# The opening stage of a two-block transformer kernel: modulation units summed in pairs per chunk on VectorE and GpSimd, sine arguments kept in PSUM, the first norm made chunk by chunk, the first two weight blocks interleaved

## The chip, the cores and the metric

One core of a Trainium2 chip runs the whole program. The metric is the device time of one execution in microseconds (us); three executions of the kernel before gave 2504.7, 2506.18 and 2512.43, median 2506.18.

## The reference, cut to what matters

Two transformer blocks run one after the other on 256 tokens of width 1024. Everything that the change touches lies ahead of the first large product:

```
mod   = silu(c) @ w_ada + b_ada                       # 9 x 1024 numbers; shift, scale, gate, ...
h     = x * rsqrt(mean(x*x) + eps) * norm_ffn1        # first RMS norm
h     = h * (1 + scale) + shift                       # modulate
x     = x + 0.5 * gate * ((silu(h @ w_g) * (h @ w_u)) @ w_down)
...
h     = sin(freq * (emb @ fw1 + fb1)); h = sin(freq * (h @ fw2 + fb2)); h = sin(freq * (h @ fw3 + fb3))
taps  = (h @ fw4) * window                            # filter of the second block's long convolution
```

## The kernel before

Features lie on the partitions: x is eight chunks of 128 features by 256 tokens (tile X). All 290 weight blocks go through one pipeline with two slots. SyncE loads block n into `raw[n % 2]`, ScalarE copies it to `whi` (the high part, `hi_static` and `hi_loop`), VectorE or GpSimd writes `wlo = raw - whi` (`lo_static`, `lo_loop`, `block_lo`), and TensorE makes three products per chunk and half (`three`: whi x Yh, whi x Yl, wlo x Yh). A block of the first product, `b1_gu1` (22 blocks), is 8 chunks x 2 halves x 3 = 48 matmuls of 256 columns into `pg[n % 2]`. The semaphore `lo_ready` counts finished low parts, `pe_block` finished blocks on TensorE, `dve_evac` evacuated ones. Block n + 2 is loaded once the low part of block n is done, and TensorE begins it once its low part is done and block n is evacuated.

The modulation vector is made in units: a unit is 128 of its numbers, a 128x1024 load of w_ada (tile ADA in the opening, `ada` later), multiplied by silu(c) spread over the partitions (bank px[1], with a copy CS in SBUF for GpSimd, which doesn't reach PSUM) and summed along the row. Units 0 to 7 are the shift and 8 to 15 the scale of the first norm, one per chunk. Sixteen units are loaded and summed in the opening: twelve on VectorE (`first_units`, one instruction and a small addition), four multiplied on GpSimd and summed on ScalarE (`unit_sum`). `ada_used` counts the units that are done, and SyncE waits for it before it loads unit 16 and later ones. In the queue of SyncE the load of unit 16 stands directly ahead of the load of weight block 2, and unit 17 ahead of block 3.

Order in the opening before: TensorE spreads silu(c), makes three small filter layers (`pe.matmul` into pg[0]; VectorE reduces each sine's argument to within pi in tile FA, ScalarE takes the sine), eight sums of squares, the filter's last layer (4 matmuls of 512 columns, weights FW4), the spread of the inverse root, and then blocks 0 and 1 one after the other. VectorE sums its twelve units between the sine arguments, weights the taps (tile HN), makes the low part of block 0, and after all units the eight chunks of the norm: a scaled chunk in TMP, the high part YhB on ScalarE, the low part YlB on VectorE. Each engine works through its own list in the written order.

Of the kernel before, what the change touches and what calls it, by code (L numbers as in the profile page):

```python
# [20 lines left out]
P = 128  # L21
D = 1024
SEQ = 256
N_FF = 2816
KD = D // P
KF = N_FF // P
EPS = 1e-6
F32 = mybir.dt.float32
# [49 lines left out]
POOL_UNITS = (9, 11, 12, 13)  # L78
DVE_UNITS = (0, 1, 2, 3, 4, 5, 6, 7, 8, 10, 14, 15)
# [112 lines left out]
def two_blocks(nc, x_t, ctx_t, vec, w_t, w_d, w_ada, emb_t, fw1, fw23, fw4, window, dft, rope1, sgu_w, sgu_b,  # L192
# [59 lines left out]
    at[0] = region + 43776  # L252
    ADA0 = sb("ADA0", [P, 11, KD * P])
    ADA1 = nc.alloc_sbuf_tensor_at("ADA1", [P, 4, KD * P], F32, offset=y_at)
    ADA2 = nc.alloc_sbuf_tensor_at("ADA2", [P, KD * P], F32, offset=yl_at)

    def first_unit(n):
        if n < 11:
            return ADA0[:, n, :]
        return ADA1[:, n - 11, :] if n < 15 else ADA2[:, :]  # L260

# [74 lines left out]
    with ExitStack() as ctx:  # L336
# [49 lines left out]
        def _(sp):  # L386
# [8 lines left out]
            for n in range(ADA_FIRST):  # L395
                sp.dma_start(first_unit(n), w_ada[n, :, :]).then_inc(sem[f"ada_first{n // 2}"], 16)
# [50 lines left out]
            def load(name):  # L447
# [26 lines left out]
                if not rate:  # L474
                    with sp.Fori(0, blocks // 2) as j:
                        weights(j, 0)
                        weights(j, 1)
                    return
# [24 lines left out]
        def _(pool):  # L503
# [66 lines left out]
            for k, n in enumerate(POOL_UNITS):  # L570
                if k == 0:
                    pool.wait_ge(sem["c_kept"], 1)
                pool.wait_ge(sem[f"ada_first{n // 2}"], 32)
                pool.tensor_tensor(first_unit(n), first_unit(n), CS[:, :], ALU.mult).then_inc(sem["pool_unit"], 1)
            pool.dma_start(DF0, dft[:, 0:2].rearrange("p a b n -> p (a b) n")).then_inc(sem["dft_in"], 16)
            pool.wait_ge(sem["taps_used"], 1)
            pool.wait_ge(sem["lo_ready"], CREDIT + 2)
# [8 lines left out]

            def block_lo(n):

                pool.wait_ge(sem["hi_ready"], n + 1)
                for q in range(4):  # L590
                    part = slice(512 * q, 512 * q + 512)
                    ins = pool.tensor_tensor(wlo[:, n % 2, part], raw[:, n % 2, part], whi[:, n % 2, part].bitcast(F32), ALU.subtract)
                ins.then_inc(sem["lo_ready"], 1)
# [66 lines left out]
        def _(act):  # L660
# [49 lines left out]
            def norm(name, chunks_of, tokens, shift, post, following=None):  # L710

                r, base, k = NORMS[name]
                if name not in SUMMED_NORMS and name != "b1_0":
# [10 lines left out]
                if name == "b1_0":  # L724
                    unit_sum(2)
                    hi_static(0, BLK)
                    unit_sum(3)
                    hi_static(1, BLK)
# [74 lines left out]

            for t, src in ((EMB, emb_t), (FW1, fw1), (FW23, fw23)):
                act.dma_start(t[:], src).then_inc(sem["filter_in"], 16)
            act.dma_start(FW4[:], fw4).then_inc(sem["fw4_in"], 16)
            act.dma_start(X[:, 0:4, 0:256], x_t[:, 0:4, :]).then_inc(sem["x_in"], 16)
            act.dma_start(X[:, 4:8, 0:256], x_t[:, 4:8, :]).then_inc(sem["x_more_in"], 16)
# [3 lines left out]
            act.dma_start(WIN[:], window).then_inc(sem["window_in"], 16)  # L812
            act.wait_ge(sem["c_spread"], 1)
            act.activation(CS[:, :].rearrange("p (a n) -> p a n", a=2), px[1][:, :, :], ACT.Copy).then_inc(sem["c_kept"], 1)

            def unit_sum(k):

                n, total = POOL_UNITS[k], small[:, 40 + k:41 + k]
# [3 lines left out]
                act.activation(MOD[:, n, 0:1], total, ACT.Identity, bias=V[:, VEC["b_mod"] + n:VEC["b_mod"] + n + 1])\  # L822
                    .then_inc(sem["unit_done"], 1)
# [6 lines left out]
            for layer in range(3):  # L830
                act.wait_ge(sem["sine_arg"], layer + 1)
# [2181 lines left out]
```

## Time and profile before

| | |
|---|---|
| time of the runs (median of 3) | 2506.18 us |
| span of the profiled execution, first to last instruction | 2496.1 us |
| what lies around the span, by that median | 10.1 us |
| TensorE busy | 2414.6 us (97%) |
| VectorE, ScalarE, GpSimd busy | 1516.9, 892.0, 380.6 us |
| first matmul of weight block 0 | at 48.6 us |

The profile has no total of its own for the profiled execution beside its span; the difference to the median of the runs is taken as what lies around the span. A time "at 48.6 us" is counted from the span's start. A row of the timeline gives start, duration, engine, source line, operation and tiles; in brackets stands how long the engine was idle before it, and what released it.

### The profile page before, as it was taken

To read this page: it belongs to the slowest core of one execution; us is meant where nothing else is said; L and a number is where in the kernel's file an instruction comes from. 1 tells how busy PE (TensorE), PEld (TensorE's weight loads), DVE (VectorE), ACT (ScalarE), POOL (GpSimd) and SP (SyncE) were. 2 spreads that over 40 slices of the span, in tenths; PEclk is the share of its full clock that TensorE was granted. 3 is DMA by queue.
4 is the path that set the end of the run, shared out by engine and by line. 5 is a ranking of instruction groups with operands and counts; after the bars stand their busy time and mean duration, and the time that the engine had idled before them with its cause. 6 is when DMAs were issued, how large, how long until landed. Compare 5 with 4: busy or idle time off the path is not lost.

```text
span 2496.1 us, 39335 instructions
## 1 busy us (share of the span) xinstructions
PE 2414.6 (97%) x14736; PEld 2134.7 (86%) x14736; DVE 1516.9 (61%) x2434; ACT 892.0 (36%) x1103; POOL 380.6 (15%) x353
## 2 busy tenths in 40 slices
PE   5998989999999998999999999999999999999999
PEld 4998879999888888867788888888888889999999
DVE  7767768977878665355478776652222274565544
ACT  3443554454222223432232222242222241344443
POOL 2110531211111102332201110101111000000110
PEclk9999989999999999999999999999999999999999
DMA  7878736854655554211125555522222342125455
GB/s 267 282 265 284 266 133 212 276 197 169 219 183 195 181 168 147 81 64 51 68 102 205 189 178 189 178 87 101 97 80 91 103 147 83 68 102 186 168 182 171
DMA packets 79878, 400.19 MB, mean 160 GB/s; under 512 B 8816, under 2 KB 12912, under 8 KB 54704
## 3 DMA queue, kind: packets, MB, share of 16 engines
q1 hardware_dynamic: 77216, 393.39, 45.6%
q0 software_dynamic: 1056, 3.67, 0.5%
q10 hardware_dynamic: 1520, 1.95, 0.2%
q8 instruction: 58, 0.95, 0.2%
q14 instruction: 28, 0.23, 0.0%
HBM read 396.88 MB, written 2.10 MB: 160 GB/s over the span
## 4 chain that ended last, share of the span: by engine, by line
PE 78%; DVE 9%; DMA 4%; issue 4%; ACT 4%; POOL 0%; DVEq 0%; ACTq 0%; SPq 0%; POOLq 0%
PE pg L1183 22%; PE pg L1184 22%; PE pg L1185 22%; DMA raw<-w_t 2%; PE pg L1360 2%; PE pg L1361 2%; PE pg L1362 2%; DMA raw<-w_d 2%; DVE wlo L2074 1%; ACT whi L691 1%; PE px L2002 1%; DVE wlo L2079 1%; ACT whi L686 1%; DVE ada L2114 1%; PE px L1763 1%
## 5 line engine op out<-in xcount | busy, mean ns | idle before, releaser
L2079 DVE TENSOR_TENSOR wlo<-raw,whi 128x2048 fp32r<-128x2048 f32 (+1 forms) x202 | 415.6, 2057 | 502.0 <-ACT whi L691 502.0
L691 ACT ACTIVATE whi<-raw 128x2048 fp32r<-128x2048 f32 (+1 forms) x202 | 348.8, 1727 | 540.1 <-PE pg L1185 487.3
L1183 PE MATMUL pg<-Yh,whi 128*128 128x512 f32 (+1 forms) x1352 | 515.8, 382 | 10.6 <-DVE Yl L2302 2.6
L1184 PE MATMUL pg<-Yl,whi 128*128 128x512 f32 (+1 forms) x1352 | 510.9, 378 | 0.0
L1185 PE MATMUL pg<-Yh,wlo 128*128 128x512 f32 (+1 forms) x1352 | 510.8, 378 | 0.0
L1183 PE MATMUL pg<-YhB,whi 128*128 128x256 f32 (+1 forms) x1504 | 435.9, 290 | 20.4 <-DVE YlB L2234 7.7
L1184 PE MATMUL pg<-YlB,whi 128*128 128x256 f32 (+1 forms) x1504 | 429.6, 286 | 0.0
L1185 PE MATMUL pg<-YhB,wlo 128*128 128x256 f32 (+1 forms) x1504 | 429.3, 285 | 0.0
L1183 PEld LDWEIGHTS pg<-YhB,whi 128*128 128x128 f32 x1504 | 287.3, 191 | 30.2 <-issue 15.8
L1183 PEld LDWEIGHTS pg<-Yh,whi 128*128 128x128 f32 x1352 | 254.2, 188 | 65.5 <-issue 6.2
L1185 PEld LDWEIGHTS pg<-Yh,wlo 128*128 128x128 f32 x1352 | 254.3, 188 | 47.2
L1184 PEld LDWEIGHTS pg<-Yl,whi 128*128 128x128 f32 x1352 | 254.4, 188 | 46.6
L1185 PEld LDWEIGHTS pg<-YhB,wlo 128*128 128x128 f32 x1504 | 287.3, 191 | 2.9
L1184 PEld LDWEIGHTS pg<-YlB,whi 128*128 128x128 f32 x1504 | 286.4, 190 | 3.0
L2114 DVE CUSTOM_DVE_ANT_0 ada<-ada,px 128x1024 f32<-128x1024 f32 x200 | 243.7, 1219 | 14.8 <-DMA ada<-w_ada 9.4
L1183 PE MATMUL pg<-Hh,whi 128*128 128x512 f32 (+1 forms) x594 | 217.8, 367 | 0.0
L1184 PE MATMUL pg<-Hl,whi 128*128 128x512 f32 (+1 forms) x594 | 217.0, 365 | 0.0
L1185 PE MATMUL pg<-Hh,wlo 128*128 128x512 f32 (+1 forms) x594 | 217.0, 365 | 0.0
L2074 DVE TENSOR_TENSOR wlo<-raw,whi 128x2048 fp32r<-128x2048 f32 (+1 forms) x65 | 132.9, 2044 | 110.8 <-ACT whi L686 110.7
L686 ACT ACTIVATE whi<-raw 128x2048 fp32r<-128x2048 f32 (+1 forms) x63 | 107.7, 1709 | 231.5 <-PE pg L1185 109.1
L550 POOL TENSOR_TENSOR Hl<-TMP,Hh 128x512 f32 x66 | 85.3, 1292 | 686.7 <-ACT Hh L706 686.7
L1183 PE MATMUL pg<-HhB,whi 128*128 128x256 f32 x528 | 148.1, 280 | 6.5 <-DVE wlo L2079 4.6
(378 smaller groups left out, 3660.3 us busy)
## 6 DMA issues: line engine op xcount, KB each, us to landing
raw<-w_t SPq DMA_DIRECT2D x194, 1024.0 KB, 5.0
ada<-w_ada SPq DMA_DIRECT2D x200, 512.0 KB, 3.6
raw<-w_d SPq DMA_DIRECT2D x96, 704.0 KB, 4.1
ADA<-w_ada SPq DMA_DIRECT2D x16, 512.0 KB, 14.3
NB<-na_bias POOLq DMA_DIRECT2D x8, 256.0 KB, 3.0
X<-x_t ACTq DMA_DIRECT2D x2, 512.0 KB, 16.3
spectrum<-HF POOLq DMA_DIRECT2D x1, 1024.0 KB, 10.1
X<-ctx_t SPq DMA_DIRECT2D x1, 1024.0 KB, 8.1
```

The source lines that it names most:

```text
L550: pool.tensor_tensor(inner_lo[:, bass.ds(j * 2 + u, 1), 0:tokens], TMP[:, u:u + 1, 0:tokens], inner_hi[:, bass.ds(j * 2 + u, 1), 0:tokens] ...
L686: act.activation(whi[:, n % 2, 0:size], raw[:, n % 2, 0:size], ACT.Copy).then_inc(sem["hi_ready"], 1)
L691: act.activation(whi[:, n % 2, 0:size], raw[:, n % 2, 0:size], ACT.Copy).then_inc(sem["hi_ready"], 1)
L1183: pe.matmul(out, w_hi, y_hi, start=first, stop=False)
L1184: pe.matmul(out, w_hi, y_lo, start=False, stop=False)
L1185: return pe.matmul(out, w_lo, y_hi, start=False, stop=last)
L1360: pe.matmul(out, y_hi, w_hi, start=first, stop=False)
L1361: pe.matmul(out, y_hi, w_lo, start=False, stop=False)
L1362: return pe.matmul(out, y_lo, w_hi, start=False, stop=last)
L2074: dve.tensor_tensor(wlo[:, n % 2, 0:size], raw[:, n % 2, 0:size], whi[:, n % 2, 0:size].bitcast(F32), ALU.subtract)\
L2079: dve.tensor_tensor(wlo[:, n % 2, 0:size], raw[:, n % 2, 0:size], whi[:, n % 2, 0:size].bitcast(F32), ALU.subtract)\
L2114: summed(dve.tensor_tensor_reduce(w, w, px[2 - streams][:, :, :], 1.0, 0.0, ALU.mult, ALU.add, total[:, streams - 1:streams]), 1 if stream ...
```

## The change

The opening is written anew; the later stages are the same, apart from line numbers. In the opening:

- The sixteen units are loaded in pairs, unit 8 + c with unit c for chunk c, with one semaphore for a pair; x is loaded ahead of them from the queue of SyncE (before: from that of ScalarE); weight blocks 0 and 1 are loaded behind pairs 3 and 4 (before: behind all units).
- GpSimd multiplies six units (before four), VectorE sums ten (before twelve). The gain (1 + scale) x norm_ffn1 is folded into each unit's small addition.
- The sine argument stays in the PSUM bank `pg[0]` (before: tile FA in SBUF). One table load is moved to the program's start and one more is added.
- The filter's last layer is copied from PSUM by ScalarE (twice 128x1024) and weighted later by GpSimd, which does it after all sixteen units; before VectorE did both in one.
- Scaled chunk, high part and low part of the norm are made chunk by chunk between the units, and GpSimd makes the low part of block 1.
- TensorE does chunks 0 to 3 of block 0, chunks 0 to 3 of block 1, and then each later chunk for both blocks.

```diff
-POOL_UNITS = (9, 11, 12, 13)
-DVE_UNITS = (0, 1, 2, 3, 4, 5, 6, 7, 8, 10, 14, 15)
+POOL_UNITS = (1, 10, 3, 13, 5, 7)
+DVE_UNITS = (8, 0, 9, 2, 11, 12, 4, 14, 6, 15)
...
-            for n in range(ADA_FIRST):
-                sp.dma_start(first_unit(n), w_ada[n, :, :]).then_inc(sem[f"ada_first{n // 2}"], 16)
+            sp.dma_start(X[:, 0:4, 0:256], x_t[:, 0:4, :]).then_inc(sem["x_in"], 16)
+            sp.dma_start(X[:, 4:8, 0:256], x_t[:, 4:8, :]).then_inc(sem["x_more_in"], 16)
+            for c in range(8):
+                for n in (8 + c, c):
+                    sp.dma_start(first_unit(n), w_ada[n, :, :]).then_inc(sem[f"ada_first{n % 8}"], 16)
+                if c in (3, 4):
+                    u = c - 3
+                    sp.dma_start(raw[:, u, :], w_t[u, :, :]).then_inc(sem[f"raw{u}_in"], 16)
...
+            pool.wait_ge(sem["lo_ready"], CREDIT + 1)
+            block_lo(1)
+            pool.wait_ge(sem["taps_copied"], 2)
+            pool.wait_ge(sem["filter_more_in"], 32)
+            pool.wait_ge(sem["ada_used"], ADA_FIRST + CREDIT)
...
+            first_sine(1)
             unit_sum(1)
-            first_square(6)
-            first_square(7)
-            act.preload_act_table(ACT.Sqrt)
+            unit_sum(10)
+            first_hi(0)
+            first_sine(2)
+            first_hi(1)
+            hi_static(0, BLK)
+            first_hi(2)
+            act.wait_ge(sem["filter_sum"], 4)
+            for tt in range(2):
+                act.activation(HN[:, tt, :].rearrange("p (a n) -> p a n", a=2), pg[tt][:, :, :], ACT.Copy).then_inc(sem["taps_copied"], 1)
+            unit_sum(3)
+            hi_static(1, BLK)
+            first_hi(3)
...
+            pe.wait_ge(sem["taps_copied"], 2)
+            pe.wait_ge(sem["lo_ready"], CREDIT + 1)
+            first_block(0, range(0, 4))
+            pe.wait_ge(sem["lo_ready"], CREDIT + 2)
+            first_block(1, range(0, 4))
+            for kt in (4, 5, 6, 7):
+                first_block(0, (kt,))
+                first_block(1, (kt,))
+
+            product("b1_gu1", 2)
...
+            first_units(6, 15)
+            first_lo(6)
+            first_scale(7)
+            first_lo(7)
             dve.wait_ge(sem["unit_done"], 2 * len(POOL_UNITS))
-            dve.sem_inc(sem["ada_sum"], len(POOL_UNITS))
-            dve.sem_inc(sem["ada_used"], len(POOL_UNITS))
+            dve.sem_inc(sem["ada_sum"], ADA_FIRST - len(DVE_UNITS))
+            dve.sem_inc(sem["ada_used"], ADA_FIRST - len(DVE_UNITS))
```

The list of VectorE at the end of the opening, before: the last unit (three rows, ADA), the low part of block 0, and then the norm's chunks (TMP scaled, YlB low part). The GpSimd units are added to `ada_used` between the low part and the small gain instruction on MOD.

```order
L2088 ISA ADA_86,small<-ADA_86,px 128x1024
L2088 ISA small 128x1
L2090 TENSOR_SCALAR MOD<-small,V 128x1
L2074 TENSOR_TENSOR wlo<-raw,whi 128x2048
L2136 SCALAR_TENSOR_TENSOR MOD<-MOD,V 128x8
L2243 SCALAR_TENSOR_TENSOR TMP<-X,MOD,px 128x256 x2
L2234 SCALAR_TENSOR_TENSOR YlB<-TMP,MOD,YhB 128x256
L2243 SCALAR_TENSOR_TENSOR TMP<-X,MOD,px 128x256
```

The same place now, from unit 6 on (tile FIRST; unit 15 lies in `ada`). The GpSimd units are added to `ada_used` behind the last row but one.

```order
L2165 ISA FIRST,small<-FIRST,px 128x1024
L2165 ISA small 128x1
L2168 TENSOR_SCALAR MOD<-small,V 128x1
L2165 ISA ada,small<-ada,px 128x1024
L2165 ISA small 128x1
L2170 TENSOR_SCALAR MOD<-small,V 128x1
L2508 SCALAR_TENSOR_TENSOR YlB<-TMP,MOD,YhB 128x256
L2502 SCALAR_TENSOR_TENSOR TMP<-X,MOD,px 128x256
L2508 SCALAR_TENSOR_TENSOR YlB<-TMP,MOD,YhB 128x256
L349 UNCONDITIONAL_BRANCH
```

So the last low part of the norm now stands ahead of the count that lets unit 16 be loaded; before it stood behind it.

The list of ScalarE in the middle of the opening now (FS the sines, FIRST the GpSimd units that it sums, YhB the high parts of the norm's chunks, HN the copied filter layer):

```order
L858 ACTIVATE YhB<-TMP,MOD 128x256
L835 ACTIVATE FS<-pg 64x256
L858 ACTIVATE YhB<-TMP,MOD 128x256
L706 ACTIVATE whi<-raw 128x2048
L858 ACTIVATE YhB<-TMP,MOD 128x256
L885 ACTIVATE HN<-pg 128x1024 x2
L842 ACTIVATE FIRST,small<-FIRST 128x1024
L845 ACTIVATE MOD<-small,V 128x1
L706 ACTIVATE whi<-raw 128x2048
L858 ACTIVATE YhB<-TMP,MOD 128x256
```

The high parts of the chunks stood in one piece at the end before (YhB x8); now chunk 3's stands behind the two copies HN, one GpSimd unit and the high part of block 1.

The queue of SyncE behind the opening's loads is the same in both, here now: unit 16, block 2, unit 17, block 3.

```order
L386 ISA
L386 DMA ada<-w_ada 128x1024
L470 REGISTER_ALU
L471 ISA
L471 DMA raw<-w_t 128x2048
L385 REGISTER_ALU
L386 ISA
L386 DMA ada<-w_ada 128x1024
```

Each load waits at the ISA row ahead of it, the first for `ada_used`, that of block 2 for `lo_ready`. Nothing moved here but the time at which the first wait ends.

## Rows read from the trace of the kernel before

**Rows 1.** The timeline of TensorE in the opening: start, duration, tiles, [idle before, releaser].

```profile
6.70 3.78 PE L1191 MATMUL px<-ident,cact 128*128 128x128 f32 x16 [6.70 <-ACT cact L810]
...
30.21 7.19 PE L1500 MATMUL pg<-FW,FS 64*128 64x512 f32 x8 [5.08 <-ACT FS L832]
```

**Rows 2.** One stretch: us; PE, PEld, DVE, ACT, POOL busy; clock, DMA share, GB/s.

```profile
74.60:160.00 85.40, 84.88 (x729) 84.71 (x730) 60.73 (x78) 39.95 (x47) 11.89 (x16) 1.00 0.81 280
```

**Rows 3.** The timeline of SyncE's queue and of the engines around blocks 2 and 4.

```profile
46.09 0.34 SPq L390 DMA_DIRECT2D ada<-w_ada  x1
46.95 0.33 SPq L468 DMA_DIRECT2D raw<-w_t  x1
...
56.73 1.92 ACT L691 ACTIVATE whi<-raw 128x2048 fp32r<-128x2048 f32 x1 [1.33 <-PE pg L1185]
...
58.69 2.88 DVE L2079 TENSOR_TENSOR wlo<-raw,whi 128x2048 fp32r<-128x2048 f32 x1 [0.24 <-ACT whi L691]
61.49 0.41 DVE L2187 TENSOR_TENSOR TMP<-SQ,pg 128x256 f32<-128x256 f32 x1
...
62.44 0.28 PE L1183 MATMUL pg<-YhB,whi 128*128 128x256 f32 x1
...
74.58 0.36 PE L1183 MATMUL pg<-YhB,whi 128*128 128x256 f32 x1 [1.09 <-DVE TMP L2187]
```

**Rows 4.** DMA issues at 46.95, 57.00 and 61.74 us: last column, us to landing.

```profile
raw<-w_t SPq DMA_DIRECT2D x1, 1024.0 KB, 7.6
raw<-w_t SPq DMA_DIRECT2D x1, 1024.0 KB, 4.9
raw<-w_t SPq DMA_DIRECT2D x1, 1024.0 KB, 7.9
```

**Rows 5.** The timeline of VectorE in the opening.

```profile
11.64 0.54 DVE L2405 TENSOR_SCALAR FA<-pg,V 64x256 f32<-64x256 f32 x1 [10.62 <-PE pg L1493]
12.21 0.29 DVE L2407 TENSOR_SCALAR FK<-FA 64x256 f32<-64x256 f32 x1
...
12.85 1.32 DVE L2410 SCALAR_TENSOR_TENSOR FA<-FK,FA 64x256 f32<-64x256 f32 x3
...
21.32 1.21 DVE L2088 CUSTOM_DVE_ANT_0 ADA<-ADA,px 128x1024 f32<-128x1024 f32 x1
...
23.91 3.39 DVE L2410 SCALAR_TENSOR_TENSOR FA<-FK,FA 64x256 f32<-64x256 f32 x3
27.33 2.38 DVE L2411 TENSOR_SCALAR FA<-FA 64x256 f32<-64x256 f32 x1
...
46.90 0.87 DVE L2243 SCALAR_TENSOR_TENSOR TMP<-X,MOD,px 128x256 f32<-128x256 f32 x2
```

**Rows 6.** The timeline of GpSimd: a unit, the taps, a block's low part.

```profile
27.22 2.35 POOL L574 TENSOR_TENSOR ADA<-ADA,CS 128x1024 f32<-128x1024 f32 x1 [1.10 <-DMA ADA<-w_ada]
...
56.97 6.91 POOL L579 TENSOR_TENSOR HP<-HN 128x1024 f32<-128x1024 f32 x2 [21.61 <-DVE wlo L2074]
...
263.65 5.01 POOL L592 TENSOR_TENSOR wlo<-raw,whi 128x512 fp32r<-128x512 f32 x4 [2.74 <-ACT whi L906]
```

**Rows 7.** The timeline of ScalarE in the opening.

```profile
41.12 1.04 ACT L820 ACTIVATE ADA<-ADA 128x1024 f32<-128x1024 f32 x1
...
42.49 1.89 ACT L686 ACTIVATE whi<-raw 128x2048 fp32r<-128x2048 f32 x1
```

**Rows 8.** DMA issues: the fourth unit (issued between 3 and 4 us).

```profile
ADA<-w_ada SPq DMA_DIRECT2D x2, 512.0 KB, 9.2
```

**Rows 9.** The chain that ended last, around 53.6 us: start, us, what.

```profile
53.44 0.21 PE pg L1183
...
53.83 0.12 PE pg L1185
```

**Rows 10.** A wait of TensorE (timeline), and a stretch behind it (clock 0.50).

```profile
389.98 0.61 PE L1368 MATMUL pg<-ones,TMP 128*128 128x1 f32 x4 [2.21 <-POOL TMP L518]
...
392.00:393.00 1.00, 0.56 (x2) 0.50 0.47 188
```

More of the change, by code:

```diff
@@ L477, in load @@
                         weights(j, 1)
+                    return
+                if name == "b1_gu1":
+                    with sp.Fori(0, blocks // 2 - 1) as j:
+                        units(j, 0)
+                        weights(j, 2)
+                        units(j, 1)
+                        weights(j, 3)
+                    units(blocks // 2 - 1, 0)
+                    units(blocks // 2 - 1, 1)
                     return
@@ L712, in norm @@
                 r, base, k = NORMS[name]
-                if name not in SUMMED_NORMS and name != "b1_0":
+                if name not in SUMMED_NORMS:
                     for c in range(k):
@@ L1494, in _, with first_block @@
                           EMB[:, :] if layer == 0 else FS[:, layer - 1, :], start=True, stop=True).then_inc(sem["filter_sum"], 1)
-            first_sums(0, 4)
+            def first_block(u, chunks):
+                for kt in chunks:
+                    pe.wait_ge(sem["y_lo"], kt + 1)
+                    for half in range(2):
+                        w = slice(256 * kt + P * half, 256 * kt + P * half + P)
+                        last = three(pg[u][:, half, 0:256], whi[:, u, w], wlo[:, u, w], YhB8[:, kt, 0:256], YlB8[:, kt, 0:256], kt == 0, kt == 7)
+                if kt == 7:
+                    last.then_inc(sem["pe_block"], 1)
+            pe.wait_ge(sem["cact_ready"], 1)
+            pe.wait_ge(sem["const_in"], 16)
+            spread([(1, 0)])
+            pe.wait_ge(sem["ones_ready"], 1)
+            pe.wait_ge(sem["filter_in"], 48)
+            filter_layer(0)
+            first_sums(0, 4)
+            filter_layer(1)
+            first_sums(4, 8)
+            turn_back("b1_0", 256)
+            filter_layer(2)
+            pe.wait_ge(sem["rms_ready"], 1)
             pe.wait_ge(sem["sine_ready"], 3)
-            pe.wait_ge(sem["fw4_in"], 16)
+            pe.wait_ge(sem["filter_more_in"], 32)
             for tt in range(2):
@@ L2400, in _, with sine_argument @@
             c3 = two_pi - c1 - c2
-            for layer in range(3):
+            link(dve.tensor_scalar(small[:, 28:36], V[:, VEC["b_mod"] + 8:VEC["b_mod"] + 16], 1.0, None, ALU.add))
+            dve.tensor_tensor(small[:, 28:36], small[:, 28:36], V[:, VEC["norm_ffn1"]:VEC["norm_ffn1"] + 8], ALU.mult)\
+                .then_inc(sem["small_ready"], 1)
+            def sine_argument(layer):
+                arg = pg[0][0:64, 0, 0:256]
                 dve.wait_ge(sem["filter_sum"], layer + 1)
```

214 lines of the change are left out of this document (124 added, 90 removed).

## The prediction

> **What bounds the kernel now.** The page's busy shares come first: TensorE 97%, so what counts is when it has work. From 74.6 to 160 us it idles only 0.5 of 85.4 us [rows 2]; a shift of the first product at block 4 is therefore carried to the end, and the whole change is priced by when block 4 begins: now at 74.58 us [rows 3]. Then the timelines of the opening. Block 0 starts at 48.6 us, and until then TensorE does small things at the lower of its two levels (1.2 GHz). The clock column says 1.00 there, but the spacing tells: 0.21 us for 256 columns up to 53.65 us, 0.12 behind it [rows 9]. The one that matters most is what ends last for block 2. Its load is issued at 46.95, just behind that of unit 16 at 46.09 [rows 3], and takes 7.6 us [rows 4], so it lands at 54.55. ScalarE takes it at 56.73, 2.2 us later, since it waits for TensorE to be done with block 0 [rows 3]. From there high part, low part and evacuation end at 61.90, and block 2 starts at 62.44, right behind block 1 [rows 3]. So the load of block 2 now has 2.2 us to spare, and no more. Blocks 0 and 1 fill TensorE meanwhile.
>
> **The change, part by part: the start.** The table load and the filter loads go first on ScalarE, so silu(c) is done some 2.1 us earlier. Spread (3.78) and first filter layer then end near 9.5, and VectorE starts its first sine argument at 9.5 instead of 11.64 [rows 1, 5]. The first pair of units: x (1 MB) now stands ahead in the same queue, so the pair ends where the fourth unit ended, landed 9.2 us after an issue between 3 and 4 us [rows 8]: 12.5, when VectorE needs it at 13. Every later pair comes 2.6 us after the last (1 MB at some 400 GB/s, an estimate from 16 units and two blocks that now end near 37), the last near 36.5: never the last thing waited for.
>
> **Sine arguments in PSUM.** An operation that reads PSUM took 0.54 us where one in SBUF took 0.29, and the three subtractions 1.32 [rows 5]. Two of seven operations go from 0.29 to 0.54, three from 0.44 to about 0.50 (the 128x256 scaling that reads a bank takes 0.44 a piece [rows 5]): 3.4 us an argument instead of 2.8, between 2.8 and 4.0. What is taken away is a stretch: beside GpSimd's unit the three took 3.39 instead of 1.32, and the next operation 2.38 instead of 0.29 [rows 5], together 4.2 us.
>
> **VectorE's work.** Three arguments 10.2; ten units at 1.38 (1.21 and the small addition) 13.8; reciprocal 0.2; sixteen chunk operations at 0.44, 7.0; low part of block 0, 2.25: 33.5 us. Without any wait the list would end at 43.
>
> **The waits that I add, by walking the five lists with these durations.** (a) The third filter layer stands behind the spread of the inverse root on TensorE, and that behind VectorE's reciprocal: 1.9 us idle, third argument done at 26.7. (b) The sine ends at 28.2; the last filter layer takes 7.19 [rows 1], to 35.4. ScalarE then does two copies (1.0 each), unit 3 (1.4) and the high part of block 1 (1.83, start to start) before chunk 3 [rows 7]: chunk 3's high part is done at 41.2. VectorE came to its low part at 37.8: over 3 us idle. (c) Behind it five chunks remain, with units 4, 14, 6 and 15: 5 x 0.44 + 4 x 0.44 + 4 x 1.38 = 9.5 us, and about 0.8 of short waits for ScalarE. (d) GpSimd: six units at 2.35 and block 1's low part at 5.0 [rows 6] against VectorE's operations with operands in SBUF alone. In my walk these cost 0.5 to 0.8 us each in four places. Together the last low part is done at 52.4 us. The rows show the stretch for sine arguments only [rows 5]; if nothing at all were stretched, the list would end at 50.9, the lower bound of this term. If the first pair came 2 us later than I read, it would end at 54.4.
>
> The Trainium skill's page "SBUF — State Buffer", section "Who interferes with whom", says that a VectorE instruction with two SBUF inputs, or a single-source one in a two-port mode, and a GpSimd instruction that reads SBUF exclude one another for a whole instruction. By that rule the low parts are hit too; without it the time would be 1.5 us shorter. The stretched rows agree with it as far as they go; no row of before shows a low part beside a unit of GpSimd.
>
> **What hangs on 52.4.** The count that lets unit 16 go stands behind the last low part now, and ahead of all chunks before (the order of VectorE). So unit 16 is issued at 52.4 instead of 46.1 and block 2 at about 52.8 instead of 46.95. With the same 7.6 us it lands at 60.4, and with the same 5.2 us for high part, low part and evacuation (56.73 to 61.90 [rows 3]) block 2 starts at 65.7: **3.3 us later** than 62.44.
>
> **TensorE meanwhile.** Block 0's chunks 0 to 2 run from 37.5. Block 1 waits for GpSimd's low part (from 40.7, done at 46.6), and the two blocks end near 58.6, some 4 us ahead of now. This gain buys nothing: it is followed by 7 us of idleness. Nothing covers it, and it may cost: behind a wait of 2.21 us and small work the clock stood at 0.50 [rows 10], and in the opening the lower level lasted 5.0 us into block 0, 5.0 x (1 - 0.12 / 0.21), **2.3 us** of loss [rows 9]. Before it was paid in block 0; now it is paid again in block 2. Bounds: nothing, and 3.0 us, if the lower level lasted as long as the wait of 7 us. I take 2.3, the nearest row.
>
> The same is weighed by the skill's page "TensorE: Matmul & The Clock Gate", section "HAM oscillation — how this bites in real kernels": waiting on a transfer between pieces of work throws the clock back, and the next piece starts cold. By it the loss is certain; without it the sum would be 2.3 less.
>
> **What comes back.** Now block 4 waits 1.09 us [rows 3] for its load (7.9 us [rows 4]). With TensorE late, that load is in time: 65.5 + 7.9, copied when block 2 ends at 73.5, low part and evacuation by 78.3, needed at 78.9. So minus 1.1 us.
>
> **Sum.** Block 4 starts at 65.7 + 5.45 + 2.3 + 5.45 = 78.9 instead of 74.6: + 4.3 us. GpSimd's taps: two weightings (2.35 each) and 6.91 [rows 6] from 52.4 end at 64, before the first hidden chunk is there (66). The profiled span would be 2496.1 + 4.3 = 2500.4; it lies 10.1 us under the median of the runs, 2506.2, and with that 2510.5.
>
> **The rivals.**
> 1. *The load of block 2 is quicker, the clock stays up.* A load with less beside it took 4.9 us [rows 4], so block 2 could start at 63.0 and, with no clock loss, block 4 at 73.9 (then 0.7 earlier than now), if its own load lets it: 2505.5. Against it: unit 16 still runs just ahead of it, unit 17 behind. Chance 0.25.
> 2. *The opening is shorter than my walk.* If ScalarE's chain (b) and the exclusions cost nothing, VectorE ends at 45 to 47 and block 2 starts 2 to 4 us earlier than now: 2499 to 2504. It would take more than that for a gain over 0.3%: even the list without any wait, 43, gives 56.4 for block 2, and TensorE would still be at blocks 0 and 1. Chance 0.17; more than 0.3% would need something outside these sums, and I leave 0.07 of it for that.
> 3. *Slower by more.* The loads of unit 16, block 2, unit 17 and block 3 are now released within 2 us, 3 MB in one queue, where before block 3's waited until 57.0. If they share evenly, block 2 takes up to 12 us instead of 7.6: block 2 at 70.1, 2515. It decides from 3.2 us above the 7.6. For it: 61.74's load beside others took 7.9; against it: 7.9 is the most that I read here. Chance 0.13.
> 4. *The change does what it says and it shows:* earlier blocks 0 and 1 carried through. That needs block 2's load released before 46; the order of VectorE excludes it.
>
> The forecast itself, 2507 to 2513.7, has the other 0.45.
>
> **How the numbers follow.** About 0.3% (7.5 us) is what a measurement of this kernel tells from no change. Faster by more: 0.07, from rival 2. Slower by more: most of rival 3 and the upper tail of the forecast (the walk's end at 54.4 with later pairs, clock loss 3.0), 0.14. The same: 0.79. The range drops the lower part of rival 2 and the end of rival 3: 2500.5 to 2516.
>
> **What would show it.** The last low part YlB of the opening at 52.4 (right between 50.5 and 54.5); unit 16's load right behind it; the load of block 2 at 7.6 us; block 1 done near 58.6 and then a wait of about 7 us for the evacuation behind block 2's low part; 0.21 us between matmuls of block 2 for some 5 us; block 4 at 78.9; HN copies behind 35.4. Wrong if VectorE's list ends before 49, if the wait ahead of block 2 is under 3 us, or if later stages differ, which the equal lists exclude.

## The result

| | before | changed |
|---|---|---|
| median of the runs | 2505.68 us (2502.76 to 2512.91, 6 runs) | 2519.34 us (2514.91 to 2523.46, 6 runs) |
| ratio | | 1.0059, 95% interval 1.0040 to 1.0077 |
| span of the profiled execution, one each | 2496.1 us | 2513.2 us |
| TensorE busy | 2414.6 us | 2421.5 us |
| first matmul of block 0 / 2 / 4 | 48.6 / 62.44 / 74.58 us | 39.82 / 70.14 / 84.04 us |

The change made the kernel slower by 0.6%, 13.7 us; the forecast was 2510.5, 4.3 us slower, with a range up to 2516. The sign was right, the size too small by two thirds.

The changed kernel's timeline of TensorE (start, duration, engine, line, tiles, [idle before, releaser]) answers to [rows 1] and to the last rows of [rows 3]:

```profile
30.21 7.16 PE L1573 MATMUL pg<-FW,FS 64*128 64x512 f32 x8 [4.46 <-issue]
39.82 0.55 PE L1235 MATMUL pg<-YhB,whi 128*128 128x256 f32 x1 [2.44 <-ACT HN L885]
48.17 0.58 PE L1235 MATMUL pg<-YhB,whi 128*128 128x256 f32 x1 [4.17 <-DVE YlB L2508]
...
59.55 0.28 PE L1237 MATMUL pg<-YhB,wlo 128*128 128x256 f32 x1
...
70.14 0.58 PE L1235 MATMUL pg<-YhB,whi 128*128 128x256 f32 x1 [10.32 <-DVE TMP L2267]
...
84.04 0.28 PE L1235 MATMUL pg<-YhB,whi 128*128 128x256 f32 x1
```

Block 0 begins 9 us earlier and blocks 0 and 1 end at 59.8, some 2.6 us earlier. Then TensorE stands still for 10.3 us. What it waits for, in the queue of SyncE, on ScalarE and on VectorE, against [rows 3]:

```profile
57.95 0.36 SPq L386 DMA_DIRECT2D ada<-w_ada  x1
58.59 0.34 SPq L471 DMA_DIRECT2D raw<-w_t  x1
...
64.53 1.91 ACT L711 ACTIVATE whi<-raw 128x2048 fp32r<-128x2048 f32 x1 [6.93 <-DMA raw<-w_t]
66.47 3.20 DVE L2156 TENSOR_TENSOR wlo<-raw,whi 128x2048 fp32r<-128x2048 f32 x1 [2.65 <-ACT whi L711]
69.60 0.41 DVE L2267 TENSOR_TENSOR TMP<-SQ,pg 128x256 f32<-128x256 f32 x1
```

Block 2's load is issued at 58.59, 11.6 us later than before, and ScalarE now waits for it. The DMA issue at 58.59 (last column: us to landing), against [rows 4]:

```profile
raw<-w_t SPq DMA_DIRECT2D x1, 1024.0 KB, 5.8
```

It lands faster than before, in 5.8 us: rival 3's transfer of 12 us didn't happen. The load is late because VectorE's list is. VectorE's timeline, against [rows 5]:

```profile
8.59 0.54 DVE L2487 TENSOR_SCALAR pg<-pg,V 64x256 f32<-64x256 f32 x1 [4.65 <-PE pg L1544]
...
15.12 1.22 DVE L2165 CUSTOM_DVE_ANT_0 FIRST<-FIRST,px 128x1024 f32<-128x1024 f32 x1 [3.40 <-DMA FIRST<-w_ada]
...
25.79 0.54 DVE L2487 TENSOR_SCALAR pg<-pg,V 64x256 f32<-64x256 f32 x1 [2.36 <-PE pg L1544]
...
33.63 1.74 DVE L2508 SCALAR_TENSOR_TENSOR YlB<-TMP,MOD,YhB 128x256 fp32r<-128x256 f32 x1
35.29 4.43 DVE L2151 TENSOR_TENSOR wlo<-raw,whi 128x2048 fp32r<-128x2048 f32 x1
...
43.01 5.10 DVE L2508 SCALAR_TENSOR_TENSOR YlB<-TMP,MOD,YhB 128x256 fp32r<-128x256 f32 x1 [1.45 <-ACT YhB L858]
...
57.63 0.48 DVE L2508 SCALAR_TENSOR_TENSOR YlB<-TMP,MOD,YhB 128x256 fp32r<-128x256 f32 x1 [0.58 <-ACT YhB L858]
```

Three rows behind the sine arguments are stretched. A chunk's low part takes 0.48 us alone (the last row); at 33.63 it took 1.74 and at 43.01 it took 5.10. Block 0's low part takes 2.3 us alone and took 4.43. GpSimd's timeline, against [rows 6], shows what lay beside them:

```profile
32.74 4.83 POOL L586 TENSOR_TENSOR FIRST<-FIRST,CS 128x1024 f32<-128x1024 f32 x2 [7.75 <-DMA FIRST<-w_ada]
...
41.91 0.96 POOL L587 DMA_DIRECT2D DF<-dft  x1
42.89 4.93 POOL L594 TENSOR_TENSOR wlo<-raw,whi 128x512 fp32r<-128x512 f32 x4
...
57.94 4.72 POOL L604 TENSOR_TENSOR HN<-HN,WIN 128x1024 f32<-128x1024 f32 x2 [10.12 <-DVEq L2546]
```

The low part of chunk 3 started 0.12 us behind GpSimd's four pieces of block 1's low part and ended 0.3 us behind the last of them: the four pieces held it to their end, not one piece. The stretch of the three rows is 1.3 + 2.1 + 4.6 = 8.0 us. A series doesn't always hold that long: the low part at 33.63 also met two multiplications back to back (the row x2 at 32.74), and it was through at 35.37, 0.3 us behind the end of the first. What differs is taken up with the arguments in SBUF below.

The weighting of the taps runs from 57.94 to 67.53 us (two multiplications HN, two instructions HP), so it also lies beside the low part of block 2, which takes 3.20 us instead of the 2.29 that it takes alone.

The stretches of the changed kernel around the wait (us; PE, PEld, DVE, ACT, POOL busy; granted clock, DMA share, GB/s):

```profile
64.00:76.00 12.00, 5.86 (x27) 5.86 (x28) 8.49 (x8) 5.08 (x6) 4.51 (x4) 0.50 0.79 289
77.00:84.00 7.00, 7.00 (x64) 7.00 (x63) 3.24 (x3) 2.60 (x3) 0.00 (x0) 1.00 0.54 204
```

The clock fell to 0.50 (1.2 GHz) in the wait and stayed there until 76 us, 6 us into block 2.

### The profile page after: what moved, and what is told of

Its sections match the earlier page's. It is cut to its first block, busy times and chain, and to the rows that moved or that the text cites. A ratio compares the mean times of both kernels' runs of the same rounds, so it can differ in the third digit from the quotient of the medians.

```text
span 2513.2 us, 39342 instructions
## 1 busy us (share of the span) xinstructions
PE 2421.5 (96%) x14736; PEld 2142.3 (85%) x14736; DVE 1516.1 (60%) x2426; ACT 897.2 (36%) x1111; POOL 394.5 (16%) x361
## 4 chain that ended last, share of the span: by engine, by line
PE 79%; DVE 8%; issue 5%; DMA 4%; ACT 3%; POOL 0%; DVEq 0%; SPq 0%; ACTq 0%; POOLq 0%
PE pg L1235 22%; PE pg L1236 22%; PE pg L1237 22%; DMA raw<-w_t 2%; PE pg L1412 2%; PE pg L1413 2%; PE pg L1414 2%; DMA raw<-w_d 1%; DVE wlo L2151 1%; PE px L2080 1%; ACT whi L711 1%; ACT whi L706 1%; DVE wlo L2156 1%; DVE ada L2194 1%; PE px L1841 1%
## 5 line engine op out<-in xcount | busy, mean ns | idle before, releaser
L1235 PE MATMUL pg<-Yh,whi 128*128 128x512 f32 (+1 forms) x1352 | 516.6, 382 | 10.5 <-DVE Yl L2379 2.6
L1235 PE MATMUL pg<-YhB,whi 128*128 128x256 f32 (+1 forms) x1504 | 438.8, 292 | 30.0 <-DVE TMP L2267 10.9
```

Source lines behind the costliest of these rows:

```text
L1235: pe.matmul(out, w_hi, y_hi, start=first, stop=False)
```

## The experiments

In each, the kernel before ran on the same chip. The times of starts (us) of the same few matmuls, counted from the program's end in each trace, so that they are the same work (block 2 and 4 of the first product; then, named by how many matmuls are left, a place early in the second product, four later ones, and the last matmul), one profiled execution each:

```
kernel                 block 2  block 4   -13542   -12870   -12630   -12438   -1302    last
before                    62.4     74.6    184.4    278.8    311.4    343.4  2345.3  2493.0
before, again             60.2     72.3    183.0    280.8    315.0    345.9  2349.7  2498.6
before, unit 16 late      63.1     77.0    183.1    282.4    314.9    346.8  2343.5  2496.2
changed                   70.1     84.0    190.1    290.2    328.3    361.0  2361.0  2510.1
changed, again            69.7     82.5    188.6    285.6    323.1    356.4  2362.7  2515.9
e1 early release          65.0     78.1    184.2    280.8    317.8    350.6  2355.5  2503.3
e3 block 1 on VectorE     67.8     81.3    187.4    286.9    320.0    353.7  2355.0  2508.2
e4 84 idle matmuls        70.6     82.0    192.2    288.9    321.5    353.5  2357.1  2504.8
f4 first pair ahead       69.9     82.7    192.9    291.8    325.0    359.4  2364.8  2512.7
f3 combined               62.8     75.9    182.0    282.5    315.1    349.1  2352.0  2505.3
g1 not interleaved        70.8     84.1    190.2    290.2    328.3    361.7  2365.0  2512.5
g2 arguments in SBUF      70.7     83.9    194.2    290.7    328.2    361.5  2362.4  2511.7
```

### Controls: both kernels again

Nothing is edited.

> The kernel before, unchanged, timed against itself: a control for the scatter. Both theories expect a ratio of 1.000, with an interval that is about 0.001 to 0.002 wide on either side. Its profile gives a second set of stretches of low granted clock. Theory A (the later loss of the changed kernel, 7 to 11 us between 225 and 360 us, is mostly scatter of the clock between executions) expects that two executions of this kernel differ by 3 to 6 us at the start of the same matmul around 360 us. Theory B (the loss belongs to the change) expects less than 2 us between them at 250 us, at the first norm's edge, and the 0.9 us wait for the square there again.

> The changed kernel, unchanged, on this chip beside the others: ratio 1.005 to 1.006 as before. Theory A expects another execution whose lag behind the kernel before at 265 us is well below the 11.6 us of the first (6 to 8), and low clock elsewhere. Theory B expects the lag at 190 us between 5 and 7 us again, then at least 9 us at 265 us, with the wait of the norm's sums for ScalarE's square at 2 to 3 us as in the first (2.8 us), because VectorE's low part of the prefetched block and one unit stand ahead of the last chunk there, and that block lands late.

The kernel before against itself: 1.0004 (0.9991 to 1.0018). The changed one: 1.0063 (1.0047 to 1.0079). Two executions of one kernel lie up to 6 us apart at the same matmul. Against both executions of before, the two of the changed kernel are 9.8 us late at block 4 on average, 5.7 at -13542, and pair by pair 8.1 to 16.9 at -12630. So there is scatter, but a later loss, between -13542 and -12630, is there in every pair. Neither theory of the first control came out cleanly: the two executions of before differ by 2.0 us at -12870 and by 2.5 at -12438, where one theory said 3 to 6 and the other less than 2.

### The release alone, on either kernel

The changed kernel with unit 16 loaded without its wait, and blocks 2 and 3 released by the low parts of 0 and 1:

```diff
-                    with sp.Fori(0, blocks // 2 - 1) as j:
-                        units(j, 0)
-                        weights(j, 2)
-                        units(j, 1)
-                        weights(j, 3)
+                    sp.dma_start(ada[:, 0, :], w_ada[ADA_FIRST, :, :]).then_inc(sem["ada0_in"], 16)
+                    weights(0, 2)
+                    weights(0, 3)
+                    units(0, 1)
+                    with sp.Fori(0, blocks // 2 - 2) as j:
...
```

> The changed kernel, but unit 16 is loaded in the opening without a wait (its slot is free) and weight blocks 2 and 3 are loaded right when blocks 0 and 1 have their low parts; only unit 17 and later wait for the sixteen units. Theory 1 (late release of block 2's load is the loss): block 2 starts at 62 to 65 us instead of 70.1, the wait ahead of it is under 5 us instead of 10.3, and the time falls by 5 to 10 us against the changed kernel, to 2509 to 2514 or ratio 1.001 to 1.003 to before. Theory 2 (the loss lies in stages after 85 us or in the order of the opening's loads, and the wait only overlaps it): block 2 starts earlier but the time stays within 3 us of 2519.

Measured 1.0060 (1.0043 to 1.0077). In the trace block 2 starts at 65.04 and block 4 at 78.12, 5.9 us earlier than in the changed kernel and 4.4 earlier than in its second execution: the late release is a cause of the opening's loss. Block 4 is still 3.5 us later than in one execution of before and 5.8 later than in the other. What lies there is again GpSimd. VectorE's and GpSimd's timelines of this kernel:

```profile
60.86 3.70 DVE L2160 TENSOR_TENSOR wlo<-raw,whi 128x2048 fp32r<-128x2048 f32 x1 [1.20 <-ACT whi L715]
...
67.28 4.82 DVE L2160 TENSOR_TENSOR wlo<-raw,whi 128x2048 fp32r<-128x2048 f32 x1 [0.84 <-ACT whi L715]
...
74.94 2.29 DVE L2160 TENSOR_TENSOR wlo<-raw,whi 128x2048 fp32r<-128x2048 f32 x1 [0.91 <-ACT whi L715]
```

```profile
57.69 4.73 POOL L608 TENSOR_TENSOR HN<-HN,WIN 128x1024 f32<-128x1024 f32 x2 [10.11 <-DVEq L2550]
62.50 6.75 POOL L611 TENSOR_TENSOR HP<-HN 128x1024 f32<-128x1024 f32 x2
```

Beside the weighted taps the low parts of blocks 2 and 3 take 3.70 and 4.82 us, alone 2.29. The first of them was through 2.1 us behind the end of HN at 62.42, with HP right behind it: here too VectorE got its turn before a series was over. The forecast of the time, 1.001 to 1.003, was missed: the median didn't fall with block 4. It doesn't refute the gain either, since each ratio is known to 0.0017 and the difference of two to some 0.0025, 6 us.

The kernel before with the wait alone, so that unit 16 comes behind the last low part:

```diff
+                if name == "b1_gu1":
+                    weights(0, 1)
+                    sp.wait_ge(sem["y_lo"], 8)
+                    units(0, 0)
+                    weights(0, 2)
...
```

> The kernel before, with one wait added on SyncE: unit 16 (and with it block 2's load behind it) is loaded only after the eight low parts of the first norm, near 54.6 us instead of 46.1. Theory 1: the slack of 2.2 us is overrun by some 6 us, block 2 starts near 68 to 69 instead of 62.4, TensorE waits 6 us there and falls to its lower level; time 5 to 9 us above before, ratio 1.002 to 1.0035. Theory 2: the late release costs nothing in itself, ratio within 0.9985 to 1.001.

Measured 1.0017 (1.0006 to 1.0028). Unit 16 goes at 52.13 instead of 46.09, TensorE waits 3.02 us, and block 4 comes at 77.0, 2.4 us later than in one and 4.7 later than in the other execution of before. That is less than expected (block 2 at 63.1, not 68 to 69), since the wait ended 6.0 us later and not 8.5, and the block then landed in 5.7 us instead of 7.6 and got its low part in 2.29 instead of 2.88:

```profile
63.13 0.55 PE L1194 MATMUL pg<-YhB,whi 128*128 128x256 f32 x1 [3.02 <-DVE TMP L2198]
```

From block 2 to block 4 it needs 13.9 us, where both executions of before need 12.1: the wait of 3 us was followed by the lower clock.

### Block 1's low part on VectorE

```diff
-            pool.wait_ge(sem["lo_ready"], CREDIT + 1)
-            block_lo(1)
...
             first_scale(4)
+            lo_static(1, BLK)
             first_units(4)
```

> The changed kernel, but the low part of block 1 is made by VectorE behind the scaling of chunk 4, not by GpSimd. Theory 3 (GpSimd's four instructions hold off VectorE's low part of chunk 3, 5.1 us instead of 0.5): that low part falls to 0.5 to 1 us, VectorE has 2.3 us more work, the last low part comes 2 to 3 us earlier (55 to 56 instead of 58) and the time falls by 2 to 3 us against the changed kernel. Theory 1 alone says the same by the same amount as the last low part moves. If the exclusion were no cause, the last low part would come 2.3 us later and the time rise by 2 us.

Measured 1.0041 (1.0026 to 1.0055). VectorE takes on 2.28 us of work and its list ends 2.3 us earlier:

```profile
43.10 0.48 DVE L2506 SCALAR_TENSOR_TENSOR YlB<-TMP,MOD,YhB 128x256 fp32r<-128x256 f32 x1 [1.48 <-ACT YhB L856]
...
43.90 2.28 DVE L2149 TENSOR_TENSOR wlo<-raw,whi 128x2048 fp32r<-128x2048 f32 x1
...
55.30 0.48 DVE L2506 SCALAR_TENSOR_TENSOR YlB<-TMP,MOD,YhB 128x256 fp32r<-128x256 f32 x1 [0.58 <-ACT YhB L856]
```

4.62 us of waiting for GpSimd are gone and 2.28 of work come in: 2.33 us. Block 2 and block 4 follow by 2.4 and 2.8 us (1.9 and 1.3 against the second execution).

### A clock kept up

84 matmuls of 256 columns into a bank that nobody reads then, ahead of block 2:

```diff
+            for i in range(84):
+                pe.matmul(px[0][:, 0, 0:256], YhB8[:, 0, 0:P], YhB8[:, 1, 0:256], start=True, stop=True)
             product("b1_gu1", 2)
```

> The changed kernel with 84 extra matmuls of 256 columns into an unused bank between block 1 and block 2 (9.6 us at the upper level), whose results nobody reads; no other work is changed. Theory 4 (the wait also costs the clock): blocks 2 and 3 run at the upper level from the start, block 4 starts 2.5 to 3.5 us earlier than 84.0, time 2 to 4 us below the changed kernel. If the clock costs nothing: time the same or up to 1 us longer.

Measured 1.0041 (1.0027 to 1.0055). Block 2 starts no earlier, and at full speed:

```profile
59.96 10.24 PE L1586 MATMUL px<-YhB 128*128 128x256 f32 x84
70.59 0.38 PE L1235 MATMUL pg<-YhB,whi 128*128 128x256 f32 x1 [0.40 <-DVE TMP L2269]
```

From block 2 to block 4 it needs 11.4 us, which is 96 matmuls at 0.118 us. The changed kernel needed 13.9 and, again, 12.8, where 96 at its spacing of 0.113 us take 10.9: the clock's fall cost 3.0 and 1.9 us. Block 4 comes only 2.0 and 0.5 us earlier, since block 2 starts 0.5 and 0.9 us later here and this execution ran at the slower of the two spacings of matmuls that are taken up below.

### The first pair ahead of x

```diff
-            sp.dma_start(X[:, 0:4, 0:256], x_t[:, 0:4, :]).then_inc(sem["x_in"], 16)
-            sp.dma_start(X[:, 4:8, 0:256], x_t[:, 4:8, :]).then_inc(sem["x_more_in"], 16)
             for c in range(8):
                 for n in (8 + c, c):
                     sp.dma_start(first_unit(n), w_ada[n, :, :]).then_inc(sem[f"ada_first{n % 8}"], 16)
+                if c == 0:
+                    sp.dma_start(X[:, 0:4, 0:256], x_t[:, 0:4, :]).then_inc(sem["x_in"], 16)
+                    sp.dma_start(X[:, 4:8, 0:256], x_t[:, 4:8, :]).then_inc(sem["x_more_in"], 16)
```

> The changed kernel with units 8 and 0 issued ahead of the two loads of x on SyncE. What is tested is the term that was set at 12.5 us for the first pair's landing and came out at 15.1: 1 MB of x stood ahead of it. If the rate of the queue sets it (x's first half took 6.7 us from issue), the pair lands at 10.5 to 12 us, VectorE's wait of 3.4 us goes to under 1, and the last low part moves from 57.6 to 55 to 56.5; then the time falls by 1.5 to 3 us, ratio 1.0045 to 1.005 where the kernel itself has 1.0059. The rival: the squares on ScalarE now wait for x, hold the first sine behind them, and the third filter layer gives the 2 us back, so that the last low part stays within 0.7 us of 57.6 and the ratio with it.

Measured 1.0071 (1.0055 to 1.0087). The rival held: the wait changed its name, not its end.

```profile
15.01 1.22 DVE L2166 CUSTOM_DVE_ANT_0 FIRST<-FIRST,px 128x1024 f32<-128x1024 f32 x1 [3.17 <-ACT CS L865]
```

VectorE now waits for ScalarE's copy of silu(c), which stands behind the squares, which wait for x. The last low part starts at 57.47.

### The interleaving undone

```diff
-            first_block(1, range(0, 4))
-            for kt in (4, 5, 6, 7):
-                first_block(0, (kt,))
-                first_block(1, (kt,))
+            first_block(0, range(4, 8))
+            first_block(1, range(0, 8))
```

> The changed kernel with block 0's eight chunks first and block 1's eight after them, as the kernel before had it. Theory 1 (block 2's load sets when block 2 starts, so the interleaving buys nothing): block 1 now ends 5.3 to 5.6 us after the last low part of 57.6, at about 64 us instead of 59.8, still ahead of block 2's low part at 69.6, and block 2 starts at 70 us again; TensorE waits 5 to 6 us instead of 10.3, so its stretch of low clock is shorter and block 4 comes 0 to 2 us earlier; ratio 1.0045 to 1.0063. Rival (the interleaving is worth what it hides): block 2 starts 4 us later, ratio 1.0075 or more.

Measured 1.0039 (1.0025 to 1.0052). Blocks 0 and 1 are done 6 us later, and block 2 starts at 70.82 all the same, behind a wait of 4.13 us:

```profile
70.82 0.58 PE L1235 MATMUL pg<-YhB,whi 128*128 128x256 f32 x1 [4.13 <-DVE TMP L2265]
```

The interleaving buys nothing here. Block 4 comes at 84.1, as in the changed kernel, so the small gain in the median isn't from the opening; its interval overlaps that of the changed kernel.

### The sine arguments in SBUF

```diff
-                act.activation(FS[:, layer, :], pg[0][0:64, 0, 0:256], ACT.Sin).then_inc(sem["sine_ready"], 1)
+                act.activation(FS[:, layer, :], FA[:, :], ACT.Sin).then_inc(sem["sine_ready"], 1)
...
-                arg = pg[0][0:64, 0, 0:256]
+                arg, psum = FA[:, :], pg[0][0:64, 0, 0:256]
...
-                link(dve.tensor_scalar(arg, arg, vcol("ffn_vec", layer, 64), ...
+                link(dve.tensor_scalar(arg, psum, vcol("ffn_vec", layer, 64), ...
```

> The changed kernel with the sine arguments kept in SBUF (FA), as the kernel before had them. Theory 1: what PSUM buys is that the argument's operations are not held up by GpSimd. Without GpSimd beside it an argument is 0.3 us shorter in SBUF (2.75 against 3.05 us: the first, and the third, which fell beside no GpSimd work), but the second lies beside GpSimd's first two units (17.6 to 22.4 us), where the kernel before had 3.4 us for three operations of 1.3 and 2.4 us for one of 0.3; it should take 5 to 7 us instead of 3.9, and the last low part should come 1 to 3 us later, ratio 1.006 to 1.007. Rival: the second argument costs no more than 0.5 us extra, VectorE's list is 0 to 0.5 us shorter, and PSUM has cost time: ratio 1.005 to 1.006 and the last low part at 57 us.

Measured 1.0049 (1.0030 to 1.0069). The second argument, beside two units of GpSimd, takes 8.3 us to the start of the next unit; in the changed kernel it took 3.9, of which 1.11 were for the one operation with both ends in SBUF:

```profile
17.89 1.60 DVE L2488 TENSOR_SCALAR FK<-FA 64x256 f32<-64x256 f32 x1
19.52 2.45 DVE L2489 TENSOR_SCALAR FK<-FK 64x256 f32<-64x256 f32 x1
22.01 3.35 DVE L2491 SCALAR_TENSOR_TENSOR FA<-FK,FA 64x256 f32<-64x256 f32 x3
```

The third ends 3.5 us later, but the last low part starts at 58.23, only 0.6 us later: block 1's low part on GpSimd then held less. Chunk 3's low part on VectorE and GpSimd's four pieces in this kernel:

```profile
46.53 1.21 DVE L2508 SCALAR_TENSOR_TENSOR YlB<-TMP,MOD,YhB 128x256 fp32r<-128x256 f32 x1 [2.55 <-ACT YhB L858]
```

```profile
46.19 5.15 POOL L594 TENSOR_TENSOR wlo<-raw,whi 128x512 fp32r<-128x512 f32 x4 [5.63 <-ACT whi L706]
```

It takes 1.21 us, where it took 5.10 in the changed kernel: VectorE got its turn behind the first of the four. So PSUM does keep the arguments out of GpSimd's way, and in the changed kernel that gain was eaten by the next collision. The times don't tell the two theories apart; the rows do.

It also shows that a series of GpSimd holds VectorE to its end only in some places. It did so at this chunk in both executions of the changed kernel and in four of the edited ones (5.07 to 5.11 us). In the later stages of every trace VectorE got its turn after one piece of such a series (GU at 286.36 us in the kernel before: 1.37 us instead of 0.35). In each of the six long cases GpSimd had issued its own load (tile DF, 41.91 us above) directly ahead of the four pieces, and it was in flight beside most of them; here it was issued at 39.60 and landed at 44.1, before they began. No run moves that load alone, so this is a companion and not a shown cause; it isn't the only one, since block 3's low part with early release (4.82 us, above) stood still over two GpSimd instructions, the second HP and the HlB behind it, with no such load near.

### What was learned, put together

Early release, block 1 on VectorE, first pair ahead, and 36 matmuls ahead of block 2 (the edits above together).

> The changed kernel with block 2 and 3 and unit 16 released early (as in the first experiment), the second block's low part on VectorE (as in the third), the first pair ahead of x, and 36 matmuls of no use ahead of block 2. Sum: last low part at 57.6 - 2.3 - 1.5 = 53.8 us, blocks 0 and 1 done at 56, block 2's low part 1 to 3 us behind VectorE's list, so block 2 starts at 59 to 61.5 (kernel before: 62.44), at full clock. If only the opening counts, the ratio is 0.998 to 1.001. Rival: the later stages lose 4 us and more however the opening goes (as the first experiment, which was level at 184 us and 10 us behind at the end): then 1.002 to 1.004.

Measured 1.0025 (1.0010 to 1.0041). Block 2 starts at 62.83, block 4 at 75.94: at block 4 it is 1.4 us behind one execution of before and 3.7 behind the other, and by the medians more than half of the loss is gone. The low parts of blocks 2 and 3 still lie beside the taps (3.78 and 4.84 us). It doesn't beat the kernel before; of the two forecasts, the rival's 1.002 to 1.004 holds.

## Why the prediction was wrong, step by step

- **The start.** 8.59 on VectorE instead of 9.5: right, a little better.
- **First pair.** Put at 12.5, VectorE had it at 15.1 (14.7 in the second execution). The step took the landing of the fourth unit [rows 8] for it; why the pair came later than that wasn't tested. Together with the rest up to the third argument this made 28.9 instead of 26.7: 2.2 us. As the experiment shows, the order of the queue isn't the remedy.
- **Arguments in PSUM.** 3.05 us (the first and the third) and 3.9 (the second, beside GpSimd) instead of 3.4, in the bounds.
- **The walk's chain (b).** ScalarE reached chunk 3's high part at 42.9 instead of 41.2, the filter's last layer ending at 37.4 instead of 35.4: carried over from the step ahead.
- **The exclusions (d): this step failed.** It set "0.5 to 0.8 us each in four places" (2.0 to 3.2 us, which its own lower bound of 50.9 puts at 1.5); the three rows that the trace shows cost 8.0, the last of them 4.6. From chunk 3's high part to the end of VectorE's list the prediction gave 11.2 us, of which 9.5 were work, 0.8 waits for ScalarE and so 0.9 exclusions; measured 15.1, with 4.6 in that one row, and the experiment with block 1's low part on VectorE took exactly it away. The mistake was to price a collision at less than one GpSimd instruction, where at that place VectorE got no turn between four. The Trainium skill, "SBUF — State Buffer", section "Who interferes with whom", says that the loser of the shared port pair stands still for the whole instruction. Two rows agree with it: 1.74 and 4.43 us for 0.48 and 2.3, ending 0.3 and 2.15 us behind the end of one GpSimd instruction. The row at 43.01 goes beyond it: it stood still for four, not for one.
- **The end of the list.** 58.1 instead of 52.4: 1.8 from the start and the filter, 3.9 behind them, nearly all of it (d).
- **What hangs on it.** The structure was right: unit 16 at 57.95, block 2's load right behind. Landing 5.8 us instead of 7.6, high part, low part and evacuation 5.7 instead of 5.3. Block 2 at 70.1 instead of 65.7. The taps weren't out of the way as forecast (64) but ended at 67.5, and cost block 2's low part 0.9 us. Rival 3 had named 70.1 for block 2 and 2515: the same start by another way, since its transfer of 12 us took 5.8. That is coincidence.
- **Wait and clock.** 10.3 us instead of 7. Two blocks took 13.9 us, where 96 matmuls at 0.1133 us take 10.9: a loss of 3.0 (1.9 in the second execution) against 2.3 predicted with bounds of 0 and 3.0. The mechanism was right and the size within its bounds. The Trainium skill's page "TensorE: Matmul & The Clock Gate", section "HAM oscillation — how this bites in real kernels", says that behind a wait between pieces of work the next one starts at the lower clock. The trace agrees (0.50 from 64 to 76 us), and with the wait filled the loss was gone.
- **Block 4.** 84.0 instead of 78.9, + 9.5 instead of + 4.3. With + 9.5 the prediction's own sum would have given 2515.7, at the edge of its range; the rest of the miss lies behind block 4.
- **"A shift at block 4 is carried to the end", and later stages differ not at all, "which the equal lists exclude": this failed too.** It put everything behind block 4 at nothing. The lag fell to 5.7 us at -13542 and was 10.5 to 17.6 us at -12438, with equal lists; what the runs show of it stands below.
- **"10.1 us around the span."** Wrong. In nearly every run 1.7 or 1.8 us lie around the span (2514.91 against 2513.2), in a few 2.2 to 2.4; by that, before's profiled execution was one of the fast ones, 8 us under its median. The sum happened to be right, since it was added on both sides.

**The later stages.** Between block 4 and -13542 the changed kernel needed 106.1 us twice, the kernel before 109.8 and 110.7. This isn't waiting. Stretches of 90 us in the first product at clock 1.00 (before's reaches 4 us into the second), in this order of before and of the changed kernel:

```profile
90.00:180.00 90.00, 89.48 (x766) 89.31 (x765) 62.72 (x83) 40.90 (x50) 11.88 (x16) 1.00 0.79 272
```

```profile
90.00:180.00 90.00, 90.00 (x796) 90.00 (x796) 65.09 (x82) 42.97 (x50) 12.20 (x17) 1.00 0.80 286
```

766 matmuls against 796: 117 ns and 113 ns each. The slower one ran here in both executions of before (in the first for the most part), the faster in both of the changed kernel, but it isn't the change: before with the wait alone needed 106.1 us for the same 936 matmuls, and three edits of the changed kernel (idle matmuls, first pair ahead, arguments in SBUF) 110.2. In the last stage the two spacings differ between two executions of the same changed kernel:

```profile
2350.00:2450.00 100.00, 100.00 (x885) 100.00 (x884) 46.69 (x37) 47.76 (x56) 14.04 (x19) 1.00 0.54 189
```

```profile
2350.00:2450.00 100.00, 100.00 (x852) 100.00 (x851) 45.95 (x37) 46.17 (x54) 13.38 (x18) 1.00 0.53 180
```

It is worth 4 us in the first product and 5 in the last stage, and explains much of the scatter between executions.

The second part is a loss at one place, the attention that follows the first two products, -12870 to -12630: 32.5 to 34.2 us in the three profiles of before, 38.1 and 37.5 in the changed kernel. There SyncE, ScalarE, VectorE and TensorE, changed kernel:

```profile
305.88 1.42 SPq L407 DMA_DIRECT2D raw<-w_t  x1
...
314.27 1.91 ACT L958 ACTIVATE whi<-raw 128x2048 fp32r<-128x2048 f32 x1 [3.52 <-DMA raw<-w_t]
315.56 1.22 DVE L2194 CUSTOM_DVE_ANT_0 ada<-ada,px 128x1024 f32<-128x1024 f32 x1 [3.67 <-DMA ada<-w_ada]
...
318.96 1.97 PE L1717 MATMUL pg<-SW,VG 128*64 128x128 f32 x16 [2.97 <-DVE MG L2614]
```

The same place before:

```profile
294.61 0.43 SPq L404 DMA_DIRECT2D raw<-w_t  x1
...
300.41 1.92 ACT L906 ACTIVATE whi<-raw 128x2048 fp32r<-128x2048 f32 x1 [0.82 <-DMA raw<-w_t]
...
301.65 1.22 DVE L2114 CUSTOM_DVE_ANT_0 ada<-ada,px 128x1024 f32<-128x1024 f32 x1 [1.03 <-DMA ada<-w_ada]
...
305.05 1.09 PE L1639 MATMUL pg<-SW,VG 128*64 128x128 f32 x16 [0.22 <-DVE MG L2499]
```

One issue takes 1.42 us instead of 0.43, its block is in ScalarE's hands 8.4 us later instead of 5.8, and VectorE waits 2.6 us longer for the unit behind it, with the attention's operations (MG) in its list behind that unit. TensorE waits 2.97 us instead of 0.22, and a stretch at the lower clock follows (10.2 us). It is there in both executions of the changed kernel, in early release, not interleaved and arguments in SBUF, with issues of 1.42 to 1.94 us; not in the three of before, nor in block 1 on VectorE, idle matmuls, first pair ahead and combined, all with 0.43.

The slow issue has a companion in the DMA queues. From 304 to 316 us in the changed kernel:

```profile
q1 hardware_dynamic: 557, 2.63, 65.6%
q8 instruction: 1, 0.02, 0.5%
```

The same stretch of before, 293 to 305 us, has no packet of the queue that the profile calls instruction:

```profile
q1 hardware_dynamic: 658, 3.29, 73.4%
```

That one packet of 16 KB starts at 306.01, 0.13 us into the slow issue. In all five traces with the slow issue such a packet starts 0.1 to 0.2 us into it and takes 0.93 to 1.43 us. Counted from matmul -12870, it comes at 15.8 to 16.0 us there, and at 9.0 to 9.6 and about 30 in the three of before. Where it meets another issue, that one is slow: with block 1 on VectorE the next unit's (1.09 us instead of 0.33), with the idle matmuls the next block's (1.23 instead of 0.43). So the edited programs differ in a later stage, with the same lists, in where these packets fall. No run moves a packet alone, so that it makes the issue slow is read from their coincidence, not shown.

At the next place, up to -12438, one more wait of TensorE, for ScalarE behind a late block, is 0.8 to 1.0 us in before and with the idle matmuls, and 2.3 to 3.4 in all the others.

So the 13.7 us are: about 10 at block 4 (7.9 to 11.7 by pairs of executions), and some 4 net of later waits and of the two spacings, which were seen and not explained. Of the 10, the experiments show the late release (4.4 to 5.9 us came back with it), GpSimd's hold on VectorE's list (1.3 to 2.8) and the clock (1.9 to 3.0) as causes that overlap: together they brought back 6.6 to 8.1. One profile each can't split them further, and the medians don't follow block 4 closely: early release gains there and nothing in the median.

## What to carry to other kernels

Before work is moved to the front of an in-order list, look at what the end of that list releases: here the next load hung on the last item, so TensorE had blocks 0 and 1 early and then nothing. When VectorE and GpSimd share a stage, price each collision of operands in SBUF at the rest of GpSimd's instruction at least and at the rest of its series at worst, and place VectorE's items with operands in SBUF outside of it, or give them one operand in PSUM. And put a second execution beside the first before a difference of some microseconds is explained.

## What the runs showed of the hardware that was not expected

- Matmuls of 256 columns at granted clock 1.00 have two spacings, 113 and 117 to 118 ns (796 or 766 in 90 us; 885 or 851 in 100), for hundreds of microseconds each, in either kernel.
- A chunk's low part of 0.48 us, started 0.12 us behind the start of a series of four GpSimd instructions, took 5.10 us; the same one 0.34 us behind the start of such a series took 1.21 with the arguments in SBUF.
- Operations on a PSUM operand beside GpSimd's units kept their time (1.33 us for three), those in SBUF alone took 3.35.
- An issue of a 1 MB load took 0.43 us, or 1.42 to 1.94 where a 16 KB packet of the instruction queue started 0.1 to 0.2 us into it, and its block then needed some 8 us instead of 5.8.
